# Conditioning vectors of an adaptive-norm mixer step: a weight-sliced matmul in three groups of 32-column tiles, two of them between the natural projection's tiles

## Reference, cut to what matters

```
def adaln(c, w_ada, b_ada):
    return jnp.split(jax.nn.silu(c) @ w_ada + b_ada, 6, axis=-1)

p_sh1, p_sc1, p_gt1, p_sh2, p_sc2, p_gt2 = adaln(c_prompt, w_ada[l], b_ada[l])
s_sh1, s_sc1, s_gt1, s_sh2, s_sc2, s_gt2 = adaln(c_sample, w_ada[l], b_ada[l])
h  = rmsnorm(x, g_mix_pre) * (1 + sc1) + sh1
qa, ka, va, qb, kb, vb, qi, ki, wi = split(h @ w_in)
...
y  = x + gt1 * rmsnorm(mixer, g_mix_post)
y  = y + gt2 * rmsnorm(swiglu(rmsnorm(y, g_ffn_pre) * (1 + sc2) + sh2), g_ffn_post)
```

## Time and profile before

| | us |
|---|---|
| median of 3 runs | 1935.0 |
| lowest and highest run | 1931.43 and 1936.4 |
| span of the profiled execution | 1930.9 |
| PE busy in the span | 1774.0 (92%) |
| DVE, ACT and POOL busy | 819.3, 651.9 and 139.4 |

### The profile page before, as it was taken

The page is one execution under the profiler, slowest core; times in us unless marked ns, Lnnn a source line. Parts: engine busy times, 40 slices in busy tenths (PEclk is TensorE's granted clock), DMA queues, the critical chain, the costliest instruction groups (busy, mean ns, idle before and its releaser), DMA issues. The chain is left out here.

```text
span 1930.9 us, 24858 instructions
## 1 busy us (share of the span) xinstructions
PE 1774.0 (92%) x9641; PEld 1436.4 (74%) x9641; DVE 819.3 (42%) x1606; ACT 651.9 (34%) x1188; POOL 139.4 (7%) x273
## 2 busy tenths in 40 slices
PE   7989799999889988899999399999999998999994
PEld 1145499994357865566654299999999998999994
DVE  0120166668899985455433411111111112444446
ACT  1010145545699953233322411111111111333332
POOL 1100000005211011111101100000000000000000
PEclk9999899999899979989999699999999998999997
DMA  9944531113000030000000311111111113200005
GB/s 344 302 80 50 157 77 44 45 35 110 1 1 1 2 134 22 22 22 23 23 23 25 114 56 43 43 44 54 43 43 43 45 42 148 92 0 0 0 0 204
DMA packets 98951, 123.44 MB, mean 64 GB/s; under 512 B 11402, under 2 KB 70866, under 8 KB 98838
## 3 DMA queue, kind: packets, MB, share of 16 engines
q1 hardware_dynamic: 96892, 116.88, 19.8%
q0 software_dynamic: 1984, 5.57, 0.9%
HBM read 105.44 MB, written 18.96 MB: 64 GB/s over the span
## 5 line engine op out<-in xcount | busy, mean ns | idle before, releaser
L1309 PE MATMUL ps<-h_hi,gu_hi 128*128 128x352 f32 x1056 | 341.7, 324 | 8.0 <-DVE gu_lo L1345 8.0
L1309 PE MATMUL ps<-h_lo,gu_hi 128*128 128x352 f32 x1056 | 339.3, 321 | 0.0
L1309 PE MATMUL ps<-h_hi,gu_lo 128*128 128x352 f32 x1056 | 338.9, 321 | 0.0
L918 PE MATMUL ps<-arena 128*128 128x512 f32 (+5 forms) x464 | 181.3, 508 | 35.6 <-DVE small L1110 18.2
L1309 PEld LDWEIGHTS ps<-h_hi,gu_hi 128*128 128x128 f32 x1056 | 198.8, 188 | 8.1 <-DVE gu_lo L1345 8.1
L1309 PEld LDWEIGHTS ps<-h_lo,gu_hi 128*128 128x128 f32 x1056 | 199.1, 189 | 0.0
L1309 PEld LDWEIGHTS ps<-h_hi,gu_lo 128*128 128x128 f32 x1056 | 198.5, 188 | 0.0
L1398 PE MATMUL ps<-a_hi,wd_hi 128*128 128x352 f32 x528 | 174.1, 330 | 13.9 <-DVE a_lo L1421 13.9
L905 PE MATMUL ps<-arena 128*128 128x64 f32 (+2 forms) x1280 | 165.8, 267 | 7.6 <-DVE arena L976 3.2
L1398 PE MATMUL ps<-a_lo,wd_hi 128*128 128x352 f32 x528 | 171.9, 326 | 0.0
L1398 PE MATMUL ps<-a_hi,wd_lo 128*128 128x352 f32 x528 | 171.4, 325 | 0.0
(11 more groups left out here) (172 smaller groups left out, 2611.7 us busy)
## 6 DMA issues: line engine op xcount, KB each, us to landing
arena<-in_w_ada SPq DMA_DIRECT2D x12, 2048.0 KB, 14.0
gate_raw<-in_w_gate SPq DMA_DIRECT2D x22, 512.0 KB, 3.6
up_raw<-in_w_up SPq DMA_DIRECT2D x22, 512.0 KB, 3.7
arena<-in_w_in SPq DMA_DIRECT2D x16, 512.0 KB, 3.5
hidden<-scratch_y SPq DMA_DIRECT2D x4, 2048.0 KB, 12.2
w_down_all<-in_w_down SPq DMA_DIRECT2D x3, 2560.0 KB, 23.6
arena<-in_x_prompt SPq DMA_DIRECT2D x4, 1024.0 KB, 16.1
arena<-in_w_out SPq DMA_DIRECT2D x2, 2048.0 KB, 10.9
```

The costliest lines, as they stand in the source:

```text
L918: mm = nc.tensor.matmul(ps_cols(B, s_col(s) + lo, hi - lo, r), q, key_source(t, h, lo, hi), start=True, stop=True)
L1309: mm = nc.tensor.matmul(B(3 * i + c, CH), cut[i][a][:, P * k:P * k + P], h[:, NTOK * k + CH * c:NTOK * k + CH * (c + 1)], start=(k == 0 an ...
```

## The change

The twelve chunks become three groups. A group has 2048 columns of w_ada and is multiplied slice by slice: a slice is the 128 rows `k` of all 2048 columns, one 1 MB load into one of six slots. Four matmuls take a slice, one per 512 columns, with outputs at partitions 0, 32, 64 and 96 of one bank, and the sum over the eight slices is kept in that bank. Group 0 is shift and scale of the mixer and stays in `conditioning`. Groups 1 (shift and scale of the feed-forward part) and 2 (the gates) are multiplied in `natural`, two slices behind each of the first eight tiles. SP issues the loads of slices 8 to 13 at the end of `conditioning`, and those of slices 14 to 23 in `natural` behind the strip stores. The bias comes as twelve small loads, each to two partitions. The adds of group 1 and 2, the stores to scratch memory and the loads of the feed-forward part's shift and scale move to `natural` on DVE and POOL.

```diff
-STRIPS = X + 6144
+ADA_ROWS, ADA_BIAS, STRIPS = X + 3456, X + 4992, X + 6528
+ADA_GROUPS, ADA_SLOTS = 3, 6
+def ada_column(g, j):
+    return (512 * j, 3 * D + 512 * j, (2 * D, 5 * D)[j // 2] + 512 * (j % 2))[g]
+def ada_slice(n, ins, T):
+    g, k = n // KT, n % KT
+    w = ins["w_ada"][0].rearrange("(p t) n -> p t n", t=KT)[:, k, :]
+    to = T(QA + 2 * D * (n % ADA_SLOTS), 2 * D)
+    if g < 2:
+        return to, w[:, 3 * D * g:3 * D * g + 2 * D]
+    return to.rearrange("p (s c) -> p s c", s=2), w.rearrange("p (s c) -> p s c", s=2)[:, :, 2 * D:3 * D]
+def ada_matmul(nc, pe, n, bank, ada_in, ada_mm, T, T3, B):
+    k = n % KT
+    pe.wait_ge(ada_in[n % ADA_SLOTS], 16 * (n // ADA_SLOTS + 1))
+    for j in range(4):
+        mm = nc.tensor.matmul(B(bank, 512, 2, 32 * j), T3(R_SC, KT, 2)[:, k, :], T(QA + 2 * D * (n % ADA_SLOTS) + 512 * j, 512),
+                              start=(k == 0), stop=(k == KT - 1))
+    mm.then_inc(ada_mm, 1)
+def ada_add(nc, dve, g, bank, ada_mm, ada_row, T, B):
+    dve.wait_ge(ada_mm, KT * g + KT)
+    for j in range(4):
+        nc.vector.tensor_tensor(T(ADA_ROWS + 512 * g, 512, 2, 32 * j), B(bank, 512, 2, 32 * j),
+                                T(ADA_BIAS + 512 * g, 512, 2, 32 * j), ALU.add).then_inc(ada_row, 1)
...
# conditioning, SP (instead of the loop over 12 chunks)
+            for n in range(ADA_SLOTS):
+                sp.dma_start(*ada_slice(n, ins, T)).then_inc(ada_in[n], 16)
+                if n == 1:
+                    for j in range(4):
+                        sp.dma_start(T(ADA_BIAS, 512, 2, 32 * j), ins["b_ada"][0, ada_column(0, j):ada_column(0, j) + 512].partition_broadcast(2)).then_inc(b_in, 16)
+                if n == 3:
+                    sp.dma_start(T3(x_at[0], 2, D), xp[:, 0:2, :]).then_inc(x_in[0], 16)
+            for n in range(ADA_SLOTS, KT):
+                sp.wait_ge(ada_mm, n - ADA_SLOTS + 1)
+                sp.dma_start(*ada_slice(n, ins, T)).then_inc(ada_in[n % ADA_SLOTS], 16)
+            for i in range(1, 4):
+                sp.dma_start(T3(x_at[2 * i], 2, D), xp[:, 2 * i:2 * i + 2, :]).then_inc(x_in[i], 16)
+            sp.dma_start(T(x_at[SAMPLE], D, DEC), ins["x_sample"][0]).then_inc(x_in[4], 16)
+            for g in range(1, ADA_GROUPS):
+                for j in range(4):
+                    sp.dma_start(T(ADA_BIAS + 512 * g, 512, 2, 32 * j), ins["b_ada"][0, ada_column(g, j):ada_column(g, j) + 512].partition_broadcast(2)).then_inc(b_late, 16)
             w_in = ins["w_in"][0].rearrange("(t p) n -> p t n", p=P)
             ...
                 sp.dma_start(wn[:, :, a:a + n], w_in[:, :, b:b + n]).then_inc(wnat_in, 16)
+            for n in range(KT, KT + ADA_SLOTS):
+                sp.wait_ge(ada_mm, n - ADA_SLOTS + 1)
+                sp.dma_start(*ada_slice(n, ins, T)).then_inc(ada_in[n % ADA_SLOTS], 16)
+            sp.wait_ge(b_late, 16 * 8)
...
# conditioning, POOL (one part instead of two; then the power, as before)
+            pool.wait_ge(ada_row, 4)
+            for j in range(4):
+                pool.dma_start(d_ada[:, 512 * j:512 * j + 512], T(ADA_ROWS, 512, 2, 32 * j)).then_inc(ada_out, 16)
+            pool.wait_ge(ada_out, 64)
+            for j in range(2):
+                for c in range(2):
+                    pool.dma_start(T(R_MOD + 16 * j + 8 * c, KT), d_ada[c, D * j:D * j + D].rearrange("(t p) -> p t", p=P),
+                                   allow_slow_non_contiguous=True).then_inc(mod_in, 16)
...
# conditioning, PE
+            for n in range(KT):
+                ada_matmul(nc, pe, n, 0, ada_in, ada_mm, T, T3, B)
# conditioning, DVE
+            ada_add(nc, dve, 0, 0, ada_mm, ada_row, T, B)
...
# natural, SP
             sp.dma_start(d_strip_b, view(T(STRIPS + STRIP_A, 1, HEADS), [[0, P], [1, STRIP_B]])).then_inc(strip_out, 16)
+            for n in range(KT + ADA_SLOTS, ADA_GROUPS * KT):
+                sp.wait_ge(ada_mm, n - ADA_SLOTS + 1)
+                sp.dma_start(*ada_slice(n, ins, T)).then_inc(ada_in[n % ADA_SLOTS], 16)
             sp.wait_ge(nat_mm, NT)
# natural, PE, behind each tile
                 mm.then_inc(nat_mm, 1)
+                if t < SAMPLE:
+                    for n in (KT + 2 * t, KT + 2 * t + 1):
+                        ada_matmul(nc, pe, n, 1 + n // KT, ada_in, ada_mm, T, T3, B)
             pe.wait_ge(doubled, 2 * NT)
+            pe.wait_ge(ada_row, 4 * ADA_GROUPS)
# natural, DVE, behind each tile's copies
+                if t in (4, SAMPLE):
+                    ada_add(nc, dve, 1 if t == 4 else 2, 2 if t == 4 else 3, ada_mm, ada_row, T, B)
...
# natural, POOL (new in this block)
+            for g in range(1, ADA_GROUPS):
+                pool.wait_ge(ada_row, 4 * g + 4)
+                for j in range(4):
+                    at = ada_column(g, j)
+                    pool.dma_start(d_ada[:, at:at + 512], T(ADA_ROWS + 512 * g, 512, 2, 32 * j)).then_inc(ada_out, 16)
+                if g == 1:
+                    ...
+            pool.wait_ge(ada_out, 128)
```

More of the change, by code:

```diff
@@ L191, in build @@
             result(hidden=hidden, **S)
-STRIPS = X + 6144
+ADA_ROWS, ADA_BIAS, STRIPS = X + 3456, X + 4992, X + 6528
[21 more added lines that the diff above has]
+                                T(ADA_BIAS + 512 * g, 512, 2, 32 * j), ALU.add).then_inc(ada_row, 1)
 def conditioning(ctx, nc, ins, outs, sem, T, T3, B, view, ident, d_ada, **_):
-    w_ada = ins["w_ada"][0].rearrange("(p t) n -> p t n", t=KT)
-    c_in, b_in, tab_in = sem("c_in"), sem("b_in"), sem("tab_in")
+    c_in, b_in, b_late, tab_in = sem("c_in"), sem("b_in"), sem("b_late"), sem("tab_in")
     x_in = [sem(f"x_in{i}") for i in range(5)]
-    ada_in = [sem(f"ada_in{i}") for i in range(3)]
+    ada_in = ctx.ada_in = [sem(f"ada_in{i}") for i in range(ADA_SLOTS)]
     wnat_in = ctx.wnat_in = sem("wnat_in")
     silu_done, ada_mm, ada_row = sem("silu_done"), sem("ada_mm"), sem("ada_row")
+    ctx.ada_mm, ctx.ada_row = ada_mm, ada_row
     ss_zero, ss_done, var_done, rstd_done, xn_done = (sem(n) for n in (
@@ L288, in _ @@
             pe.wait_ge(silu_done, 1)
[L289 to L301, removed]
+            for n in range(KT):
+                ada_matmul(nc, pe, n, 0, ada_in, ada_mm, T, T3, B)
+            pe.wait_ge(tab_in, 48)
+            nc.tensor.matmul(B(7, STRIP_B, HEADS), T(tab_b, HEADS, BUCKETS), T(hot_b, STRIP_B, BUCKETS),
+                             start=True, stop=True).then_inc(strip_mm, 1)
         @block.vector
@@ L305, in _ @@
             nc.vector.memset(T(R_SS, NT), 1.0).then_inc(ss_zero, 1)
[L306 to L314, removed]
             dve.wait_ge(tab_in, 48)
@@ L319, in _ @@
             nc.vector.tensor_scalar(T(strip_a + 511, 257, HEADS), view(tab, [[-1, 257]], 2 * REL), -1.0, None, ALU.mult).then_inc(strip_done, 1)
+            dve.wait_ge(b_in, 64)
+            ada_add(nc, dve, 0, 0, ada_mm, ada_row, T, B)
             dve.wait_ge(strip_mm, 1)
             nc.vector.tensor_scalar(T(strip_b, STRIP_B, HEADS), B(7, STRIP_B, HEADS), -1.0, None, ALU.mult).then_inc(strip_done, 1)
-            for c in range(3, 10):
-                ada_rows(c)
             dve.wait_ge(ss_done, NT)
@@ L329, in _ @@
                 nc.vector.tensor_scalar(T(x_at[t], D, r), T(x_at[t], D, r), T(R_RSTD + t, 1, r), None, ALU.mult).then_inc(xn_done, 1)
[L330 to L337, removed]
+            dve.wait_ge(mod_in, 96)
+            for c in range(2):
+                nc.vector.scalar_tensor_tensor(T(R_SCALE + 8 * c, KT), T(R_MOD + 16 + 8 * c, KT), 1.0,
+                                               T(R_G, KT), ALU.add, ALU.mult).then_inc(mod_done, 1)
 def turn_pe(nc, pe, turned, ht_act, ht_dve, x_at, T, B, ident, ready=None):
@@ L391, with natural @@
 HT_ACT, HT_DVE = 8 + KT, 8
-def natural(ctx, nc, ins, outs, sem, T, T3, B, view, ident, d_strip_a, d_strip_b, **_):
+def natural(ctx, nc, ins, outs, sem, T, T3, B, view, ident, d_ada, d_strip_a, d_strip_b, **_):
     turned, ht_act, ht_dve = sem("turned"), sem("ht_act"), sem("ht_dve")
@@ L504, in _ @@
             k_read(dve, 1, k_dve)
+            dve.wait_ge(mod_in, 64)
+            for c in range(2):
+                nc.vector.scalar_tensor_tensor(T(R_SCALE + 16 + 8 * c, KT), T(R_MOD + 32 + 16 + 8 * c, KT), 1.0,
+                                               T(R_G + 8, KT), ALU.add, ALU.mult).then_inc(mod_done, 1)
+        @block.gpsimd
+        def _(pool):
+            for g in range(1, ADA_GROUPS):
[4 more added lines that the diff above has]
+                if g == 1:
+                    pool.wait_ge(ada_out, 64)
+                    for j in range(2):
+                        for c in range(2):
+                            at = 3 * D + D * j
+                            pool.dma_start(T(R_MOD + 32 + 16 * j + 8 * c, KT), d_ada[c, at:at + D].rearrange("(t p) -> p t", p=P),
+                                           allow_slow_non_contiguous=True).then_inc(mod_in, 16)
+            pool.wait_ge(ada_out, 128)
 NCH = 3
```

19 lines of the change are left out of this document (3 added, 16 removed).

## The result

The changed kernel takes 1944.5 us in the median of four runs (1943.35 to 1946.99), against 1933.4 for the kernel before in the runs beside it. The ratio is 1.0061, with a 95% interval of 1.0045 to 1.0076: slower by 0.6%, 11 us. The forecast was 1962 us, with a range of 1945 to 1983: 27 us of loss, where 11 were measured. The direction is right; the time lies just under the range. The profiled execution has a span of 1942.7 us against 1930.9.

A forecast was written before the change was run, and what follows sets the result against it. Conditioning was taken as bound by PE, with DMA close behind; after the change, natural waits behind the strips. Sum: -50.3 (conditioning) + 27.4 (16 slices) + 50.1 (wait, landing, clock) = +27.2 us, median 1962, range 1945 to 1983.

The forecast's parts named there:

- conditioning ends earlier: Conditioning block: only group 0 stays ahead of natural, so the block ends near 55.7 us against 106.05, 50.3 less.
- seven pairs of slices: Natural, on PE: slices placed behind tiles at 1.71 us each; all 16 were put at 27.4 us, these pairs at 23.9.
- from tile 3 to tile 4: wait, slices 14 and 15, clock: Natural: PE waits near 49 us for slices 14 and 15, then pays for slice 15 and a lower clock; 53.5 in all.
- The mechanism of the wait: Natural: loads of slices 14 to 23 stand in SP's queue behind the strip stores, 96 us of queue; chance 0.50.
- The flat share: DMA under the strip stores: a share just under a half, 8 of 16 engines, expected from about 67 to 163 us.
- the price of a slice: PE, four matmuls of a slice: 1.71 us, as in-order record pairs, between bounds of 0.86 and 3.43.
- The rival, all four side by side: PE: the four column tiles of a slice overlap fully, 0.86 us a slice, median 1954 us; chance 0.20.
- The end of the strips: SP's queue: the strip stores start at 67 us when the queue is through, take 96 us and end at 163.4.
- the clock behind the wait: PE after the wait behind tile 3: the clock is at its lower level, a loss of 2.9 us.
- The costs set at nothing: SP's 36 issues, bias rows, slice slots, group-1 adds on DVE and the tail's four bias adds: hidden, no cost.
- The fast rival: Natural: loads of slices 14 to 23 pass the strips, so no wait; 1912 us (1898 to 1945), chance 0.16.
- the next rival: PE: column tiles don't overlap, a slice costs 3.43 us, slice 15 takes 2.5 more; 1978 us, chance 0.14.

The follow-up runs named there:

- The run with a plain group 0: Group 0 multiplied without column tiles, four matmuls per slice into four banks, groups 1 and 2 as in the changed kernel: 1944.4 us, ratio 1.0051.

## Why the prediction was right in its direction and wrong in its size

The forecast of natural's end was 27.2 us later, the trace says 12.3. By the forecast's parts, with slices 14 and 15 counted to the wait in which they stand:

| | predicted, us | measured, us |
|---|---|---|
| conditioning ends earlier | -50.3 | -53.7 |
| transposes and first tile at the lower clock | 0 | +4.0 |
| seven pairs of slices | +23.9 | +13.8 |
| from tile 3 to tile 4: wait, slices 14 and 15, clock | +53.5 | +48.2 |
| natural's end | +27.2 | +12.3 |

The measured pairs are the copies' distances less those of before: 117.99 - 78.07 less three tiles of 11.28, and 230.44 - 177.44 less three of them and a last one of 11.40. The row below them is 177.44 - 117.99 less one tile.

- *The mechanism of the wait was right.* The flat share, one wait behind tile 3, the tail as before, all later work shifted whole. The queue rule of the Trainium skill (DMA: Bandwidth & Descriptors, "Queues, rings and completion order") is borne out by the 42.6 us, by the 74.3 with more strips ahead, and by no wait on another queue.
- *The step that failed is the price of a slice*, taken as 1.71 us because "the records come in order" and "the second record of one tile must follow its first". It is 1.01. The rival, all four side by side at 0.86, is nearer; over it stand the 0.3 us that a pair loses at the changes from tile to pair and back (2.03 against four rounds of 0.43). The error counts in full behind the wait: there eight slices are 5.7 of the 14.9 us by which natural ends earlier than forecast, the largest part. The page of the Trainium skill that was cited (TensorE: Matmul & The Clock Gate, Part 3: Packing small matmuls — row/col tiling) gave the right side. Its 2.38 times for three column tiles becomes 3.4 times for four here: 8 records of 0.43 are 3.43 us, against 1.01. The same section of the Trainium skill also says that matmuls start strictly in order; with the order turned round a tile and its pair took 13.33 us against 13.31, so here the measurement differs.
- *The end of the strips.* Since the wait ends when they do, what came before it cancels, and the 14.9 us between forecast and trace split by the order of events, to the rounding: strips out at 159 and not 163.4, 4.4 us; slices 14 and 15 landing by 163.0, 4.0 us behind the strips and not 7.0, as half of each had moved on the free engines before, 3.0; slice 15 and the clock behind the wait, 1.7; eight later slices at 0.7 less, 5.7. The strips were early because the queue was through at 64 and not 67: the first 20 us moved 318 GB/s and not the 273 of the earlier trace rows, which is 0.9 MB or some 2.7 us, and from 40 to 64 it was 352 and not 337.
- *Conditioning* went as worked out, in each step some microseconds early: the first transpose at 52.31 against 55.7. The run with a plain group 0 shows that this does not count while the strips bound.
- *Not in the sum*: PE's 22 us of idling before natural. The granted clock has a mean of 0.77 from 52.3 to 65.1, between its two levels, and the transposes and the first tile pay 4.0: 12.77 us (52.31 to 65.08) instead of 10.15 (106.05 to 116.20), and 12.96 on the tile where the next one takes 11.55. As it comes before tile 3, this too is only exchanged for waiting.
- *The costs set at nothing* held: SP's 36 issues, the bias rows, the slots. The tail's four adds show as PE's wait of 4.0 us (before 1.1) and stay under SP's output issues; the tail grew by 0.4.
- *The fast rival* needed the loads to pass the strips and gave 1912. With another queue they do, at 1896; 16 slices at 0.7 less are 11 of the 16 us between. The upper end of its span does not follow from its terms: -50.3 + 16 x 3.43 gives 1940 and not 1945, before the slower group 0 that the next rival names. Nor do that rival's 2.5 us for slice 15, where 3.43 - 1.71 is 1.72. The forecast rests on neither.

## What to carry to other kernels

Before work is moved under another stage, ask which queue its loads stand in and what stands ahead: an idle half of the DMA engines is no help to a load that waits its turn, and a store that is read from 8 partitions can set the pace of all that stands behind it. Moving the loads to another engine's queue, or spreading the store over 16 partitions, turned a loss of 0.6% into a gain of 1.9% with the matmuls untouched. And where a price can't be read in the trace and its bounds lie a factor of four apart (0.86 and 3.43), a plausible argument for the middle is worth little: weigh the ends.

## What the runs showed of the hardware that was not expected

- Four column tiles of two columns each run their f32 records fully side by side: 16 records in four rounds of 0.43 us, in either order of issue.
- The issue of one 1 MB load held SP for 48.4 us while the strips lay ahead in its queue; the earlier trace rows show 25.4 for the second strip behind fewer bytes.
- The same 4.7 MB store runs at 50 GB/s on a share of 0.47 from SP, at 99 GB/s on 0.90 when read from 16 partitions, and from POOL at 50 GB/s on 0.88. In the last case each byte costs more engine time, and 1 MB loads beside it land in 48 us.
- Nine normalisations on DVE took 7.28 us while POOL issued four loads (42.82 to 47.03 us), and 6.04 in the runs where POOL was idle. Why was not tried.
